# Prompt self-attention that takes both heads of a pair in one step, with TensorE alternating between halves of its array

## What is computed

```python
for (window, dilation) in ((128, 1), (512, 4), (2048, 16)):
    ...
    s = jnp.einsum('bnqrhe,bnkrhe->bnrhqk', qb, kb).astype(jnp.float32) * (Dh ** -0.5)
    bias = -slopes[:, None, None] * (dist * dilation).astype(jnp.float32)
    s = jnp.where(valid[None, :, None, None], s + bias, -jnp.inf)
    m = jnp.max(s, axis=-1)
    p = jnp.exp(s - m[..., None])
    den = jnp.sum(p, axis=-1)
    num = jnp.einsum('bnrhqk,bnkrhe->bnqrhe', p, vb.astype(jnp.float32))
...
o_a = merge_by_denominator(parts)       # sum of num over sum of den, per query and head
```

## Time and profile before

| | us |
|---|---|
| median of 3 runs | 3031.09 (3028.96 to 3045.73) |
| the profiled execution | 3023.99 |
| its span | 3020.6 |
| mean granted TensorE clock in it | 0.965 |
| prompt self-attention, first scores to last output | 213.5 (1267.6 to 1481.1) |

### The profile page before, as it was taken

The page is one execution under the profiler, slowest core; times in us unless marked ns, Lnnn a source line. Parts: engine busy times, 40 slices in busy tenths (PEclk is TensorE's granted clock), DMA queues, the critical chain, the costliest instruction groups (busy, mean ns, idle before and its releaser), DMA issues.

```text
span 3020.6 us, 43956 instructions
## 1 busy us (share of the span) xinstructions
PE 2790.8 (92%) x16485; PEld 2552.3 (84%) x16485; DVE 1209.5 (40%) x2257; ACT 567.0 (19%) x1209; POOL 681.5 (23%) x379
## 2 busy tenths in 40 slices
PE   6999999999989995799987989887899999999998
PEld 4999999999979994566544979746899999999997
DVE  6322232222268995365533240622342222222224
ACT  3100000000031113454322031311211000000003
POOL 2222332222213441201000211101323222233210
PEclk8999999999999997798999999998999999999999
DMA  4111111111101222514397211463101111111101
GB/s 123 42 42 42 42 48 49 42 42 42 42 14 49 80 85 63 204 57 140 107 263 211 67 36 51 159 241 98 49 29 48 49 42 42 42 42 49 49 14 59
DMA packets 214542, 225.87 MB, mean 75 GB/s; under 512 B 11450, under 2 KB 180470, under 8 KB 210387
## 3 DMA queue, kind: packets, MB, share of 16 engines
q1 hardware_dynamic: 197479, 196.89, 21.2%
q10 hardware_dynamic: 17004, 28.21, 2.6%
HBM read 192.41 MB, written 32.67 MB: 75 GB/s over the span
## 4 chain that ended last, share of the span: by engine, by line
PE 75%; issue 9%; DVE 7%; DMA 4%; ACT 2%; PEld 1%; DVEq 1%; SPq 0%; POOL 0%; ACTq 0%; PEldq 0%; POOLq 0%
PE ps L561 20%; PE ps L563 20%; PE ps L562 20%; PE ps L751 3%; PE ps L775 2%; PE ps L765 1%; PE ps L570 1%; DVE ya L1484 1%; PE ps L856 1%; PE ps L812 1%; DMA Kw<-in_cache_win_k 1%; PE ps L963 1%; DVE hidl L1381 1%; DVE rs L1359 1%; PE ps L826 1%
## 5 line engine op out<-in xcount | busy, mean ns | idle before, releaser
L561 PE MATMUL ps<-hh,wh 128*128 128x384 f32 (+1 forms) x2688 | 881.6, 328 | 48.1 <-DVE hl L1413 29.4
L563 PE MATMUL ps<-hl,wh 128*128 128x384 f32 (+1 forms) x2688 | 880.5, 328 | 0.0
L562 PE MATMUL ps<-hh,wl 128*128 128x384 f32 (+1 forms) x2688 | 880.3, 328 | 0.0
L561 PEld LDWEIGHTS ps<-hh,wh 128*128 128x128 f32 x2688 | 508.5, 189 | 51.2 <-issue 49.8
L521 POOL CAST wh<-raw 128x1024 fp32r<-128x1024 f32 x136 | 148.4, 1091 | 1721.0 <-PE ps L563 1433.1
L562 PEld LDWEIGHTS ps<-hh,wl 128*128 128x128 f32 x2688 | 508.2, 189 | 0.0
L563 PEld LDWEIGHTS ps<-hl,wh 128*128 128x128 f32 x2688 | 508.0, 189 | 0.0
L1393 DVE TENSOR_TENSOR ht<-ps,sg 128x384 f32<-128x384 f32 x132 | 70.7, 536 | 898.7 <-PE ps L563 896.0
L523 POOL TENSOR_TENSOR wl<-raw,wh 128x1024 fp32r<-128x1024 f32 x148 | 382.1, 2582 | 92.4 <-ACT wh L1135 81.3
L561 PE MATMUL ps<-hidh,bh 128*128 128x384 f32 (+1 forms) x1056 | 346.4, 328 | 11.7 <-DVE x L1405 11.7
L1405 DVE SCALAR_TENSOR_TENSOR x<-ps,x 128x384 f32<-128x384 f32 (+1 forms) x528 | 276.4, 533 | 185.4 <-PE ps L563 185.2
(11 more groups left out here) (203 smaller groups left out, 2959.8 us busy)
## 6 DMA issues: line engine op xcount, KB each, us to landing
raw<-in_ffn_gate SPq DMA_DIRECT2D x44, 512.0 KB, 3.8
raw<-in_ffn_up SPq DMA_DIRECT2D x44, 512.0 KB, 3.8
raw<-in_ffn_down SPq DMA_DIRECT2D x44, 512.0 KB, 3.3
Kw<-in_cache_win_k SPq DMA_DIRECT2D x48, 256.0 KB, 6.4
Vw<-in_cache_win_v SPq DMA_DIRECT2D x48, 256.0 KB
raw<-in_w_in SPq DMA_DIRECT2D x20, 512.0 KB, 3.8
Kw<-in_cache_win_k SPq DMA_DIRECT2D x8, 1024.0 KB, 10.6
Vw<-in_cache_win_v SPq DMA_DIRECT2D x8, 1024.0 KB
```

The costliest lines, as they stand in the source:

```text
L561: pe.matmul(out, w_hi_, a_hi, start=first, stop=False)
L562: pe.matmul(out, w_lo_, a_hi, start=False, stop=False)
L563: return pe.matmul(out, w_hi_, a_lo, start=False, stop=last)
```

## The change

A step is now (p, t) and holds both heads of the pair: WN = 16 and WP = 8. In the code of TensorE:

- scores(n) alternates between the heads, that is between rows 0 to 63 and rows 64 to 127 of the array. Head h writes bank 2h (and 2h+1 for t of 4 and more); for t below 4 it takes bank 2h + n%2.
- values(n) alternates between columns 0 to 63 and 64 to 127, for each block of keys in turn, into the two halves of one bank.
- The order within step n is scores(n+1), turn(n, 0), values(n-1), turn(n, 1). Scores run one step of two heads ahead. Where t is 4 or more (and at t = 0) scores(n+1) waits until both heads of the step before have left PSUM, otherwise until both heads of the one before that have.

On VectorE the custom instruction of the mask now works on the negated and scaled sum with a minimum, so that its result is the exponential's bias as it stands; the instruction on line 1542 is gone, and the exponential has scale -1. Two masks, the output of the step before (now one copy of 128 partitions) and two normalisations follow one another. ScalarE's exp(n+1, h) comes behind the copies of turn(n, h). `Sb` has two buffers of two heads, `ktok` one for both pairs. Counts of semaphores follow. TensorE waits for the second pair's loads before their transposes.

```diff
-    wsteps = [(p, h, t) for p in range(2) for h in range(2) for t in range(QT)]
+    wsteps = [(p, t) for p in range(2) for t in range(QT)]
...
             def scores(n):
-                p, h, t = wsteps[n]
+                p, t = wsteps[n]
...
-                pe.wait_ge(A["s_free"], i * WN + (WN + n - 1))
+                both = t >= 4 or t == 0
+                pe.wait_ge(A["s_free"], i * (2 * WN) + (2 * WN + 2 * n - 2 * (not both)))
                 for c in range(1 + (t >= 4)):
                     w = min(512, P * (t + 1) - 512 * c)
-                    mm = pe.matmul(ps[:, 2 * (n % 2) + c, 0:w], qT[64 * h:64 * h + 64, p, t * P:(t + 1) * P],
-                                   kTp[64 * h:64 * h + 64, p, 512 * c:512 * c + w], start=True, stop=True)
+                    for h in range(2):
+                        b = 2 * h + (c if t >= 4 else n % 2)
+                        mm = pe.matmul(ps[:, b, 0:w], qT[64 * h:64 * h + 64, p, t * P:(t + 1) * P],
+                                       kTp[64 * h:64 * h + 64, p, 512 * c:512 * c + w], start=True, stop=True)
                 mm.then_inc(A["s_full"], 1)
...
                 for k in range(t + 1):
-                    mm = pe.matmul(ps[64 * h:64 * h + 64, 6 + n % 2, 0:P], vtok[:, p, k, 64 * h:64 * h + 64],
-                                   PT[:, n % 2, k, :], start=(k == 0), stop=(k == t))
+                    for h in range(2):
+                        mm = pe.matmul(ps[64 * h:64 * h + 64, 6 + n % 2, 0:P], vtok[:, p, k, 64 * h:64 * h + 64],
+                                       PT[:, n % 2, h, k, :], start=(k == 0), stop=(k == t))
                 mm.then_inc(A["o_full"], 1)
...
             for n in range(WN):
-                if n + 2 < WN:
-                    scores(n + 2)
-                turn(n)
+                if n + 1 < WN:
+                    scores(n + 1)
+                for kind, p_, half in turns(n):
+                    if kind != "p":
+                        pe.wait_ge(A[f"in{p_}"], i * 64 + 64)
+                        tokens(vT if kind == "v" else kTp, p_, half)
+                turn(n, 0)
                 if n >= 1:
                     values(n - 1)
+                turn(n, 1)
...
-                dve.tensor_tensor_reduce(out=Sb[:, n % 3, 0:w], in0=ps[:, b:b + 2, :].rearrange("p b n -> p (b n)")
-                                         [:, 0:w], in1=pb[:, p, h, SEQ - w:SEQ], scale=1.0, scalar=-3.0e38,
-                                         op0=ALU.add, op1=ALU.max, accum_out=stat[:, n % 4, 0:1]
-                                         ).then_inc(A["s_free"], 1)
-                dve.wait_ge(A["s_free"], i * WN + (WN + n + 1))
-                dve.tensor_scalar(stat[:, n % 4, 1:2], stat[:, n % 4, 0:1], -0.125, None, ALU.mult
-                                  ).then_inc(A["m"], 1)
+                dve.tensor_tensor_reduce(out=Sb[:, n % 2, h, 0:w], in0=src[:, 0:w], in1=pb[:, p, h, SEQ - w:SEQ],
+                                         scale=-0.125, scalar=3.0e38, op0=ALU.add, op1=ALU.min,
+                                         accum_out=stat[:, n % 2, h, 0:1]).then_inc(A["s_free"], 1)
...
-                dve.tensor_copy(oT[64 * h:64 * h + 64, p, t * P:(t + 1) * P], ps[64 * h:64 * h + 64, 6 + n % 2, 0:P]
-                                ).then_inc(A["o_free"], 1)
+                dve.tensor_copy(oT[:, p, t * P:(t + 1) * P], ps[:, 6 + n % 2, 0:P]).then_inc(A["o_free"], 1)
```

More of the change, by code:

```diff
@@ L309, in turns @@
     def turns(n):
-        p, h, t = wsteps[n]
-        own = [("p", c) for c in range(1 + (t >= 4))]
-        early = {WP - 2: [("v", 0), ("v", 1)], WP - 1: [("k", 0), ("k", 1)]}
+        p, t = wsteps[n]
+        own = [("p", h, c) for h in range(2) for c in range(1 + (t >= 4))]
+        early = {WP - 2: [("v", 1, 0), ("v", 1, 1)], WP - 1: [("k", 1, 0), ("k", 1, 1)]}
         return early.get(n, []) + own
@@ L1186, in tokens, with exp @@
                     act.wait_ge(A["kst"], i * 64 + (32 + 32 * p))
[L1187 to L1188 removed]
+                dst = vtok[:, p] if kind == "v" else ktok
+                evac(dst[:, 4 * half:4 * half + 4, :])
                 if half == 1:
                     act.wait_ge(A["t_free"], i * WT + (tf[0] + 2))
[L1191 to L1195, removed]
+                    act.dma_start(win_p[kind][:, :, bass.ds(i * (2 * P) + p * P, P)], dst[:]).then_inc(A["kst"], 16)
+            def exp(n, h):
+                p, t = wsteps[n]
+                act.wait_ge(A["s_free"], i * (2 * WN) + (2 * WN + 2 * n + h + 1))
                 w = P * (t + 1)
[L1197 to L1198 removed]
+                act.activation(Sb[:, n % 2, h, 0:w], Sb[:, n % 2, h, 0:w], ACT.Exp, bias=stat[:, n % 2, h, 0:1],
+                               scale=-1.0, accum_out=stat[:, n % 2, h, 1:2]).then_inc(A["e"], 1)
             def store(p):
@@ L1522, in _ @@
         A = S["pa"]
-        dve.sem_inc(A["s_free"], WN)
+        dve.sem_inc(A["s_free"], 2 * WN)
         dve.sem_inc(A["o_free"], 2)
@@ L1527, in _, with mask @@
         with dve.Fori(0, H // 4) as i:
-            def mask(n):
-                p, h, t = wsteps[n]
+            def mask(n, h):
+                p, t = wsteps[n]
                 w = P * (t + 1)
-                if n % WP == 0:
+                if n % WP == 0 and h == 0:
                     dve.wait_ge(A[f"in{p}"], i * 64 + 64)
-                dve.wait_ge(A["s_full"], i * WN + (WN + n + 1))
-                b = 2 * (n % 2)
+                if h == 0:
+                    dve.wait_ge(A["s_full"], i * WN + (WN + n + 1))
+                src = ps[:, 2 * h:2 * h + 2, :].rearrange("p b n -> p (b n)") if t >= 4 else ps[:, 2 * h + n % 2, :]
@@ L1558, in output @@
                 dve.wait_ge(A["o_full"], i * WN + (n + 1))
-                dve.tensor_copy(oT[64 * h:64 * h + 64, p, t * P:(t + 1) * P], ps[64 * h:64 * h + 64, 6 + n % 2, 0:P]
-                                ).then_inc(A["o_free"], 1)
-            mask(0)
-            mask(1)
-            normalise(0)
+                dve.tensor_copy(oT[:, p, t * P:(t + 1) * P], ps[:, 6 + n % 2, 0:P]).then_inc(A["o_free"], 1)
+            for h in range(2):
+                mask(0, h)
+            for h in range(2):
+                normalise(0, h)
             for n in range(WN):
-                if n + 2 < WN:
-                    mask(n + 2)
                 if n + 1 < WN:
-                    normalise(n + 1)
+                    for h in range(2):
+                        mask(n + 1, h)
                 if n >= 1:
                     output(n - 1)
+                if n + 1 < WN:
+                    for h in range(2):
+                        normalise(n + 1, h)
             output(WN - 1)
```

63 lines of the change are left out of this document (29 added, 34 removed).

## The result

| kernel | median, us | runs | ratio to before (95% interval) |
|---|---|---|---|
| changed, first comparison | 2966.2 | 4 | 0.9743 (0.9711 to 0.9776) |
| changed, second comparison | 2963.1 | 6 | 0.9770 (0.9745 to 0.9794) |

The account below looks back on a forecast made before the run. TensorE was taken to bound the prompt attention: 127 us of work, 20 of waits and 12 of clock make 159, say 160, instead of 213.5. That is 53.5 less, so the kernel was forecast at 2977 us, range 2960 to 3001.

Parts of the forecast that it names:

- TensorE bounds the stage, and the end with it: Prompt attention: TensorE is the bound, so its saved time comes off the end until VectorE or ScalarE is late.
- Values pair, 27.1: Values matmuls on alternating column halves run two at once, passes 0.062 us apart: 35.7 us instead of 62.8.
- Scores pair, 29.3: Score matmuls on alternating row halves run at once: 32.6 us instead of 61.9.
- Changes of form, 10.9: TensorE's switches between scores, transposes and values: four per two-head step instead of six, 20.3 us instead of 31.2.
- New waits, 20: TensorE waiting for masks and normalisations, mostly in narrow steps: 10 us an iteration, 20 in all, bounds 6 and 40.
- The removed VectorE instruction, nothing: Dropping 64 small instructions after the mask saves VectorE time, worth nothing by itself since VectorE isn't the bound.
- Clock, 12 instead of 13: Prompt attention's loss to the low granted clock: 12 us instead of 13, as both iteration starts stay unchanged.
- row halves that don't pair: Rival for scores: matmuls on different row halves don't run at once; kernel at 2997 us, chance 0.10.
- the bound on issue: Rival for values: passes limited by how fast they are issued, 0.109 us apart; kernel at 2996 us, chance 0.04.
- the softmax chain as the bound in all steps: Rival: VectorE and ScalarE bound every step, not only narrow ones; waits 40 us, kernel at 2997, chance 0.07.
- The rival of the clock: Rival: gaps in each step hold TensorE at 1.2 GHz through the stage; slower, 3051 us, chance 0.04.
- grows by what is saved here: Sign that the prediction is wrong: the sample attention behind the stage lengthens by the time saved in it.

Follow-up runs that it names:

- scores_waited: Changed kernel, but TensorE waits on a semaphore for head 0's score matmuls before starting head 1's; stage 198.6 us, median 3018.7 us, ratio 0.9939.
- after_again: The changed kernel once more, unaltered, with a second trace; stage 145.5 us, median 2963.1 us, ratio 0.9770.
- scores_apart: Changed kernel, but all score matmuls of head 0 come before those of head 1 in a step; stage 142.7 us, median 2968.1 us, ratio 0.9782.
- values_apart: Changed kernel, but all values blocks of head 0 come before those of head 1; stage 161.3 us, median 2984.1 us, ratio 0.9834.
- before_warm2: Kernel before, plus 8 unused matmuls around the stage's first DMA wait and 3 at each iteration's start; stage 205.3 us, median 3026.9 us, ratio 0.9947.

## Why the prediction was right and wrong

- **TensorE bounds the stage, and the end with it:** right. At full clock 60 of the 73 us that its work lost (194.3 to 121.1) came off the stage.
- **Values pair, 27.1:** right in kind, 4.3 too small. The pitch of 0.062 from a short run of transposes was too careful; the four-pass row had given 0.055, and 32 passes keep it. The Trainium skill's 62 ns per MATMUL ("TensorE: Matmul & The Clock Gate", section "Wait — 56ns, not 53.3ns?"), which it gives for hardware decode turned off, doesn't bind here: 0.055 was measured over 32 passes, each with a weight load. No run shows how the decode was set.
- **Scores pair, 29.3:** right, and as passes 1.6 too small (31.0 us are left of them); for the stage the pairing brought 17, since waits took the place of the rest. I let two heads' weight loads follow one another; but four passes of 128 columns take 0.49 us, 0.27 for the last, 0.105 for the first load and 0.11 for one distance. Loads on different row halves run at once as well. What the Trainium skill's same page says in the section "Part 3: Packing small matmuls — row/col tiling", that matmuls on different row groups run at once, is borne out by the row of eight passes in 1.99 us.
- **Changes of form, 10.9:** not measured alone. Together with the small instruction (2 to 4), and less the new waits that such steps bring without any pairing, it came to 15.
- **New waits, 20:** right as far as a remainder can show it. At full clock the stage is 141.1; values 31.4, scores 31.0, transposes 38.4 and changes 20.3 (my estimate, not measured) are 121.1, which leaves 20.0. TensorE has nothing in flight for 16.5 us. Some of these waits stand behind normalisations that GpSimd's work seems to stretch, which the sum didn't know.
- **The removed VectorE instruction, nothing:** too low by 2 to 4, since narrow steps wait for VectorE. It was partly contained in the 20 us of waits.
- **Clock, 12 instead of 13:** this step failed. I wrote that both low stretches "begin at the start of an iteration", whose start is unchanged, and kept their length. That they begin there was nearly right; how long the clock then stays down is not. The stage after loses 4.4 us (3% of 145.5) to the clock in both of its traces. Before, it loses 12.8 in the trace I had and 24.8 in the next. So the clock gave 8 to 20 us where I had 1.
- **The miss, added up:** the stage gained 68 us between the first two traces where the sum had 53.5. Of the difference of 15, the passes of values and scores that were priced too dear are 5.9 and the clock term is 7.6 (12 expected after, 4.4 measured); the rest is rounding. Between after and the second trace of before the gain is 80, with the clock alone adding 12 more. The whole kernels gained 70 (78 by the first ratio), which lies between. That the profiled execution stood for the median was the second half of the clock's error: it is 7.1 below it, and had the shorter low stretches of the two traces.
- **The rivals:** row halves that don't pair would have left 158 at full clock (169 with the waits that hold them apart) against 141, and is refuted. So is the bound on issue, by passes 0.053 to 0.055 apart, and the softmax chain as the bound in all steps, since the waits are 20 and not 40. The rival of the clock is refuted too: with gaps in each step the clock was up for more of the stage than before (0.97 instead of 0.94 and 0.89).
- **The sample attention "grows by what is saved here":** its growth in the first trace was of that execution.

## What to carry to other kernels

Two independent matmuls that each use half the rows or half the columns run at once if they stand near each other in TensorE's order, for up to four passes of distance here. This is worth most of what they save (28 of 31 us for values), as long as TensorE is the bound, and less when waits for the other engines take its place (17 of 31 for scores). Read the granted clock of several executions before a stage is costed: a stage that starts behind a pause can lose 3 to 11% of itself to the lower level (15% in scores_waited), by an amount that changes with what TensorE does next. When the bound engine's work falls by a third, look at once for what the next engine does between two of its waits: instructions that cost nothing before (0.15 us of VectorE, 64 times) come back on the path, and look at what another engine does beside them (here GpSimd on the next weights).

## What the runs showed of the hardware that I had not expected

- Passes on one half overtake passes on the other: 8 fully paired when ordered four and four (0.66 us), and an overlap of about four passes a half when ordered sixteen and sixteen (3.33 us instead of 1.97).
- Weight loads of 128 columns on the two row halves overlap: four passes of 128 columns with four loads in 0.49 us.
- A normalisation of 384 columns on VectorE took 0.42 us, and 2.57 when it started beside a GpSimd subtraction of 2.34 us (after_again); normalisations that run long stand beside this work of GpSimd's in every trace. No run takes the two apart.
- Behind pauses of 2.0 to 2.6 us the lower clock lasted 20 to 24 us with scores on one row half at a time and 3.4 us in scores_apart and values_apart, with scores on both; with the pause filled it didn't come (before_warm2). Why the first stretch of the kernel before was 20.5 us once and 41.0 another time stays open.
- The sample attention's 40 MB moved at 215 to 240 GB/s from one execution to the next, 167 to 187 us, whatever the kernel.
